# First transfers of a decoder layer: four of one k-tile and six of two, two of them issued by ScalarE, with joint splits and a 128-column warm-up source

## What is computed

```
h = einsum('bsd,de->bse', x, w_in)                 # x: 256 x 2048, w_in: 2048 x IN_WIDTH
q, k, v, z_attn, u_pool, z_pool, g_pre = split(h)
y_attn = mixed_dilated_attention(q, k, v) * silu(z_attn)
y_pool = causal_pool_mixer(u_pool) * silu(z_pool)
merged = sigmoid(..) * (y_attn @ w_proj_attn) + sigmoid(..) * (y_pool @ w_proj_pool)
out    = layer_norm(alpha * x + merged @ w_out)
```

## Time and profile before

| | |
|---|---|
| median of 3 runs | 939.66 us (939.53 to 940.01) |
| profiled execution | 939.67 us |
| span, first to last instruction | 937.9 us |
| TensorE busy | 930.7 us, 99% of the span |
| VectorE, ScalarE busy | 603.6 us, 399.6 us |
| mean granted TensorE clock | 0.999 |
| DMA | 180.77 MB, mean 193 GB/s |

### The profile page before, as it was taken

How to read it: one execution, slowest core, us unless ns; L and a number is a source line. 1 busy time by engine, 2 the same in 40 slices (tenths; PEclk the granted TensorE clock), 3 DMA queues, 4 the chain that set the end, 5 groups by cost and what they waited for, 6 DMA issues and landing times.

```text
span 937.9 us, 12269 instructions
## 1 busy us (share of the span) xinstructions
PE 930.7 (99%) x4838; PEld 796.9 (85%) x4838; DVE 603.6 (64%) x910; ACT 399.6 (43%) x533; POOL 0.2 (0%) x4
## 2 busy tenths in 40 slices
PE   9999999999999999999999999999999999999997
PEld 7888888888888888888888888888888888888887
DVE  6767657666777567557666768555555555556866
ACT  6444444444444344345344444444334433434340
POOL 0000000000000000000000000000000000000000
PEclk9999999999999999999999999999999999999999
DMA  9744544544545544544545546765565555557432
GB/s 375 265 158 176 207 180 150 207 162 170 204 156 181 183 174 164 202 180 155 203 160 194 185 175 244 256 227 193 180 210 195 202 179 186 203 209 257 179 135 90
DMA packets 26855, 180.77 MB, mean 193 GB/s; under 512 B 3247, under 2 KB 3503, under 8 KB 6191
## 3 DMA queue, kind: packets, MB, share of 16 engines
q1 hardware_dynamic: 25776, 173.71, 51.4%
q10 hardware_dynamic: 1028, 6.33, 1.8%
HBM read 177.93 MB, written 2.10 MB: 192 GB/s over the span
## 4 chain that ended last, share of the span: by engine, by line
PE 98%; DVE 1%; DMA 0%; ACT 0%; DVEq 0%; issue 0%
PE proj_ps L424 27%; PE proj_ps L430 14%; PE attn_ps L416 7%; PE attn_ps L417 7%; PE attn_ps L418 7%; PE value_ps L418 5%; PE value_ps L417 5%; PE value_ps L416 5%; PE proj_ps L417 3%; PE proj_ps L418 3%; PE proj_ps L416 3%; PE mixed_ps L418 3%; PE mixed_ps L417 3%; PE mixed_ps L416 3%; PE mixed_ps L553 1%; PE proj_ps L467 1%
## 5 line engine op out<-in xcount | busy, mean ns | idle before, releaser
L899 DVE TENSOR_TENSOR w_lo<-w_raw,w_hi 128x1024 fp32r<-128x1024 f32 x314 | 369.1, 1219 | 118.4 <-ACT w_hi L724 118.4
L724 ACT ACTIVATE w_hi<-w_raw 128x1024 fp32r<-128x1024 f32 x314 | 314.0, 1053 | 209.3 <-PE mixed_ps L418 76.3
L424 PE MATMUL proj_ps<-xt,w_hi 128*128 128x512 f32 x1088 | 378.9, 393 | 0.0
L430 PE MATMUL proj_ps<-xt,w_lo 128*128 128x256 f32 x1088 | 302.1, 280 | 0.0
L424 PEld LDWEIGHTS proj_ps<-xt,w_hi 128*128 128x128 f32 x1088 | 202.6, 187 | 44.1
L430 PEld LDWEIGHTS proj_ps<-xt,w_lo 128*128 128x128 f32 x1088 | 205.6, 189 | 1.4
L739 ACT ACTIVATE corr<-proj_ps 128x256 f32<-128x256 f32 x70 | 27.0, 385 | 205.8 <-PE proj_ps L430 203.0
L913 DVE TENSOR_TENSOR qk_f<-proj_ps,corr 128x256 f32<-128x256 f32 x46 | 19.5, 424 | 73.1 <-ACT corr L739 73.1
L418 PE MATMUL value_ps<-w_hi,xt 128*128 128x512 f32 x160 | 62.3, 390 | 0.0
L417 PE MATMUL value_ps<-w_lo,xt 128*128 128x512 f32 x160 | 62.3, 389 | 0.0
L416 PE MATMUL value_ps<-w_hi,xt 128*128 128x512 f32 x160 | 62.2, 389 | 0.0
(11 more groups left out here) (196 smaller groups left out, 1179.1 us busy)
## 6 DMA issues: line engine op xcount, KB each, us to landing
w_raw<-in_weights SPq DMA_DIRECT2D x158, 1024.0 KB, 4.8
first_raw<-in_first SPq DMA_DIRECT2D x8, 640.0 KB, 7.8
res<-in_x_rows ACTq DMA_DIRECT2D x1, 2048.0 KB
bias_rows<-in_gate_bias ACTq DMA_DIRECT2D x4, 512.0 KB, 4.7
out_rows<-res SPq DMA_DIRECT2D x8, 256.0 KB, 2.1
gamma<-in_gamma_row ACTq DMA_DIRECT2D x1, 1024.0 KB
beta<-in_beta_row ACTq DMA_DIRECT2D x1, 1024.0 KB
mask<-in_mask SPq DMA_DIRECT2D x1, 512.0 KB, 17.7
```

Source lines behind the costliest of these rows:

```text
L424: mm(bank, w_hi[:, slot, k * P:(k + 1) * P], tile.rearrange("p a s -> p (a s)"), start=first, stop=False)
L430: done = mm(bank[:, SEQ:2 * SEQ], w_lo[:, slot, k * P:(k + 1) * P], tile[:, 0, :], start=False, stop=last)
L724: activation(w_hi[:, slot, cols], w_raw[:, slot, cols], ACT.Copy).then_inc(hi_split, 1)
L899: tt(w_lo[:, slot, cols], w_raw[:, slot, cols], w_hi[:, slot, cols].bitcast(F32), ALU.subtract).then_inc(lo_split, 1)
```

## The change

The first transfers are cut into ten pieces: four of one k-tile (320 KB, rows of 2560 bytes) and six of two as before. Pieces 2 and 4 are issued by ScalarE, after it has waited for `zeros`, and run one activation on one column of it; the other eight are issued by SP in their order. ScalarE and VectorE split every piece jointly: one instruction for x and one of all three chunks for w. TensorE does, for the pieces of one k-tile, the w_hi matmuls of all three chunks and then their w_lo matmuls; for the pieces of two, w_hi and w_lo chunk by chunk as before, the last two pieces again chunk after chunk. The warm-up is 7 matmuls in place of 8, and each reads the same 128 columns of `zeros` four times, so that VectorE clears 128 columns and not 512.

```diff
--- before.py
+++ after.py
@@ -52,13 +52,14 @@
 RING = 3
 AHEAD = 2
 
-WARM_UP = 8
+WARM_UP = 7
 KEEP_UP = 10
 
-PIECES = tuple((k, k + 2) for k in range(0, KT, 2))
+SINGLES = 4
+BY_SCALAR = (2, 4)
+PIECES = tuple((k, k + 1) for k in range(SINGLES)) + tuple((k, k + 2) for k in range(SINGLES, KT, 2))
 ABREAST = RING
-SIDE_BY_SIDE = 6
-BY_CHUNK = 3
+SIDE_BY_SIDE = len(PIECES) - 2
 APART = (ABREAST - 1, ABREAST)
 PIECE_COLS = SEQ + ABREAST * P
 
@@ -349,28 +350,17 @@
             return piece_raw(q)[:, (upto - before) * SEQ:(upto - before) * PIECE_COLS].rearrange(
                 "p (n c) -> p n c", n=ABREAST)
 
-        def parts_of(q):
-
-            return [slice(n, n + 1) for n in range(ABREAST)] if q < BY_CHUNK else [slice(0, ABREAST)]
-
-        def x_parts_of(q):
-
-            before, upto = PIECES[q]
-            return [slice(k, k + 1) for k in range(before, upto)] if q == 0 else [slice(before, upto)]
-
-        def x_parts_done(k):
-            q = k // (PIECES[0][1] - PIECES[0][0])
-            return k + 1 if q == 0 else PIECES[0][1] + q
-
-        def parts_done(n, q):
-            return q * ABREAST + n + 1 if q < BY_CHUNK else BY_CHUNK * (ABREAST - 1) + q + 1
-
         def apart(j):
             return attn_ps[:, (j - APART[0]) * 512:(j - APART[0] + 1) * 512]
 
         def landed(eng, n, j, i, per):
 
             eng.wait_ge(raw_landed[(n + j) % RING], 16 * ((n + j) // RING) + i * (16 * per // RING))
+
+
+        def load_piece(eng, q):
+            lies = slice(P * PIECES[q][0] * PIECE_COLS, P * PIECES[q][1] * PIECE_COLS)
+            eng.dma_start(piece_raw(q), first_d[lies].rearrange("(p c) -> p c", p=P)).then_inc(piece_landed[q], 16)
 
 
         @block.sync
@@ -378,9 +368,9 @@
             def load(slot, chunk):
                 sp.dma_start(w_raw[:, slot, :], stream_d[chunk, :, :]).then_inc(raw_landed[slot], 16)
 
-            for q, (before, upto) in enumerate(PIECES):
-                lies = slice(P * before * PIECE_COLS, P * upto * PIECE_COLS)
-                sp.dma_start(piece_raw(q), first_d[lies].rearrange("(p c) -> p c", p=P)).then_inc(piece_landed[q], 16)
+            for q in range(len(PIECES)):
+                if q not in BY_SCALAR:
+                    load_piece(sp, q)
             for slot in range(RING):
                 load(slot, RING + slot)
             for dst, src in ((mask[:, :, :], mask_d), (ident[:, :], ident_d), (coef[:, :], coef_d),
@@ -461,13 +451,17 @@
             def first_part(n, q):
 
                 bank, ks = first_bank(n), range(*PIECES[q])
-                pe.wait_ge(piece_hi_done, parts_done(n, q))
+                pe.wait_ge(piece_hi_done, q + 1)
+                pe.wait_ge(x_lo_done, q + 1)
                 for k in ks:
-                    pe.wait_ge(x_lo_done, x_parts_done(k))
                     mm(bank, w_hi[:, n, k * P:(k + 1) * P], xt[:, k, :, :].rearrange("p a s -> p (a s)"),
                        start=(k == 0), stop=False)
-                pe.wait_ge(piece_lo_done, parts_done(n, q))
-                for k in ks:
+
+            def first_lo_part(n, q):
+
+                bank = first_bank(n)
+                pe.wait_ge(piece_lo_done, q + 1)
+                for k in range(*PIECES[q]):
                     done = mm(bank[:, SEQ:2 * SEQ], w_lo[:, n, k * P:(k + 1) * P], xt[:, k, 0, :],
                               start=False, stop=(k == KT - 1))
                 return done
@@ -475,11 +469,19 @@
             def first_chunks():
 
                 for q in range(SIDE_BY_SIDE):
-                    for n in range(ABREAST):
-                        first_part(n, q)
+                    if q < SINGLES:
+                        for n in range(ABREAST):
+                            first_part(n, q)
+                        for n in range(ABREAST):
+                            first_lo_part(n, q)
+                    else:
+                        for n in range(ABREAST):
+                            first_part(n, q)
+                            first_lo_part(n, q)
                 for n in range(ABREAST):
                     for q in range(SIDE_BY_SIDE, len(PIECES)):
-                        done = first_part(n, q)
+                        first_part(n, q)
+                        done = first_lo_part(n, q)
                     done.then_inc(chunk_done, 1)
 
             def scores(i):
@@ -559,7 +561,8 @@
 
             pe.wait_ge(zeros_ready, 1)
             for _ in range(WARM_UP):
-                mm(mixed_ps[:, :], zeros[:, 0:P], zeros[:, :], start=True, stop=True)
+                mm(mixed_ps[:, :].rearrange("p (a c) -> p a c", c=P), zeros[:, 0:P],
+                   zeros[:, 0:P].unsqueeze(1).broadcast_to([P, 512 // P, P]), start=True, stop=True)
             pe.sem_inc(chunk_done, FROM)
             def pool_map():
 
@@ -740,13 +743,14 @@
 
                 act.wait_ge(proj_free, FROM + banked(n, 0))
 
+            act.wait_ge(zeros_ready, 1)
+            activation(rstd[:, 4:5], zeros[:, 0:1].bitcast(F32), ACT.Copy)
+            for q in BY_SCALAR:
+                load_piece(act, q)
             for q, (before, upto) in enumerate(PIECES):
                 act.wait_ge(piece_landed[q], 16)
-                for k in x_parts_of(q):
-                    activation(xt[:, k, 0, :], piece_x(q)[:, k.start - before:k.stop - before, :],
-                               ACT.Copy).then_inc(x_hi_done, 1)
-                for n in parts_of(q):
-                    activation(w_hi[:, n, piece_cols(q)], piece_w(q)[:, n, :], ACT.Copy).then_inc(piece_hi_done, 1)
+                activation(xt[:, before:upto, 0, :], piece_x(q), ACT.Copy).then_inc(x_hi_done, 1)
+                activation(w_hi[:, :, piece_cols(q)], piece_w(q), ACT.Copy).then_inc(piece_hi_done, 1)
             act.sem_inc(hi_split, 2 * ABREAST)
 
             def exp_probs(i):
@@ -915,16 +919,14 @@
             def freed(n, j, i):
                 dve.wait_ge(proj_free, FROM + banked(n, j) + 1)
 
-            nc.vector.memset(zeros[:, :].bitcast(F32), 0.0).then_inc(zeros_ready, 1)
+            nc.vector.memset(zeros[:, 0:P].bitcast(F32), 0.0).then_inc(zeros_ready, 1)
             for q, (before, upto) in enumerate(PIECES):
-                for k in x_parts_of(q):
-                    dve.wait_ge(x_hi_done, x_parts_done(k.stop - 1))
-                    tt(xt[:, k, 1, :], piece_x(q)[:, k.start - before:k.stop - before, :],
-                       xt[:, k, 0, :].bitcast(F32), ALU.subtract).then_inc(x_lo_done, 1)
-                for n in parts_of(q):
-                    dve.wait_ge(piece_hi_done, parts_done(n.stop - 1, q))
-                    tt(w_lo[:, n, piece_cols(q)], piece_w(q)[:, n, :],
-                       w_hi[:, n, piece_cols(q)].bitcast(F32), ALU.subtract).then_inc(piece_lo_done, 1)
+                dve.wait_ge(x_hi_done, q + 1)
+                tt(xt[:, before:upto, 1, :], piece_x(q), xt[:, before:upto, 0, :].bitcast(F32),
+                   ALU.subtract).then_inc(x_lo_done, 1)
+                dve.wait_ge(piece_hi_done, q + 1)
+                tt(w_lo[:, :, piece_cols(q)], piece_w(q), w_hi[:, :, piece_cols(q)].bitcast(F32),
+                   ALU.subtract).then_inc(piece_lo_done, 1)
             dve.sem_inc(lo_split, 2 * ABREAST)
             for pad in (u_pad, pool_a, pool_b):
                 chain.add(nc.vector.memset(pad[:, 0:PAD], 0.0))
```

## The result

The changed kernel takes 941.85 us in the median of 9 runs (941.27 to 944.40), the kernel before 939.60 in 9 (939.49 to 940.01): 2.25 us more, a ratio of 1.0025 (95% interval 1.0015 to 1.0036). The slowest execution of before is 1.26 us faster than the fastest of the change, so the slowdown is real, where +0.4 us was forecast; 941.85 lies above the forecast's upper end of 941.0. The profiled execution took 941.39 us, 1.72 more than before's.

What follows compares the result with a forecast made beforehand. TensorE's progress through the first pieces was taken to bound the kernel. Piece 4 landing at 8.6 plus 4.05 gave 12.65 to 12.7 against 12.27, so 939.7 + 0.4 = 940.1 us, range 939.3 to 941.0.

Steps and rivals of the forecast that it cites:

- The bound: TensorE never idles from its first real matmul to 900 us, so delay in the first pieces moves the end equally.
- The start: First real matmul on TensorE at 5.0 us instead of 5.84, 0.8 us earlier, as the halved first piece lands at 4.1.
- L4 + 4.05: Time when TensorE is done with pieces 0 to 4: 4.05 us after piece 4 lands, against 12.27 before.
- L4: Landing time of piece 4, two k-tiles, the piece that decides; forecast 8.6 us, changing the total by L4 - 8.2 us.
- in perfect order, 8.1: Piece 4's landing if pieces arrive in order: 8.02 us plus 0 to 0.2 for smaller rows; a gain of 0.1 us.
- the meeting of the two queues: SP's and ScalarE's queues alternate packet by packet, so part of piece 5 overtakes piece 4, which lands at 8.6 us.
- the 2.5 of 8 rows assumed: Share of piece 5 taken to overtake piece 4: 2.5/8 of 1.58 us, added to 8.1.
- Order of issue: Rival, 0.12: DMA serves by issue time, piece 5 ahead of piece 4; landing 9.7 us, total 941.2, or 11.3 and 942.8.
- Warm-up at no cost: The shortened warm-up ends at 4.66 us instead of 5.40 and costs nothing while the real work is not ready.
- hides any clock trouble: TensorE's waits at piece 4 let it be late by up to 0.33 + 0.54 us before that costs anything.
- The 0.04 for slower: Chance given to a measurable slowdown of the whole kernel, beside 0.02 for faster and 0.94 for same.

Runs made afterwards that it cites:

- after_warm8: The changed kernel with 8 warm-up matmuls instead of 7: +1.93 us against the kernel before.
- sp_all: The changed kernel with all ten pieces issued by SP, none by ScalarE: +1.18 us against the kernel before.
- sp_paced: sp_all, with SP issuing a piece only when the piece four before it has landed, first weight chunks likewise: +0.22 us against the kernel before.
- odd_even: The kernel before with each of its first two pieces issued as two 320 KB transfers, even and odd partitions, rows of 5120 bytes: +0.79 us.
- small_rows: The kernel before with each of its first two pieces as one 640 KB transfer of 256 rows of 2560 bytes: +0.03 us.
- before_scalar: The kernel before, own 640 KB pieces and splits, with pieces 2 and 4 issued by ScalarE: +1.46 us.
- late_stream: sp_all, with SP waiting for piece 6 to land before issuing the first weight chunks and constants: +1.25 us against the kernel before.
- two_sp: Against the changed kernel: two one-k-tile pieces, then seven of two, all from SP, first two pairs split chunkwise, 8 warm-up matmuls: +1.31 us against the kernel before.
- halves: The kernel before with each of its first two pieces issued as two 320 KB transfers, lower and upper 64 partitions, rows of 5120 bytes: +3.00 us.

## Why the prediction was wrong

*The bound* was right: what TensorE gets through in the first pieces sets the end. Piece 5's first matmul moved by 1.77, 3.02 and 1.35 us in three profiles (the change, after_warm8, sp_all), the executions by 1.72, 2.97 and 1.23. sp_paced and odd_even ended 0.6 us earlier than that, by a stretch from 294 us on that the change does not touch.

*The start.* Forecast 5.0, measured 4.92; warm-up end 4.66 forecast, 4.78 measured.

*L4 + 4.05* held: 9.87 + 4.05 = 13.92 against 14.04.

*L4, the landing of piece 4, is the step that failed*: forecast 8.6, measured 9.87. These 1.3 us are the whole error of the profiled execution, 941.39 against 940.1. Both terms of L4 were too small.

The first is "in perfect order, 8.1". It took the stretch's 419 GB/s for transfers of half the size, with 0 to 0.2 us for the smaller rows. The rows cost nothing (small_rows), but with transfers of 320 KB single DMA engines fall behind, and in the kernels that issue everything from SP the rate falls too: 9.48 in sp_all, 1.4 us above the term. In the changed kernel late engines and supply make some 0.9 us by the landing events. The trace of before had no transfer of that size under load, so the bound from above should have been wide, and was not.

The second is the meeting of the two queues, forecast to add 0.5 us. In the changed kernel it made some 0.9 us by the landing events: as if more than half of piece 5 had gone ahead of piece 4 (0.9 of 1.58 us), not the 2.5 of 8 rows assumed. Taking it away won less, 0.4 us in the profiles, because sp_all lost more supply instead; between the medians it won 1.1. The mechanism, sharing packet by packet, is the one that was seen (before_scalar, 88 packets against 83), and it costs 1.5 us there without small transfers. ScalarE's issues went out at 1.41 and 1.83, while its table load ran, and not at 2.15 and 2.6 behind it.

*Order of issue*, the slower rival, named 9.7 for L4 and 941.2 us and came nearest in numbers, but not by its mechanism: piece 5 did not go ahead of piece 4, they moved together.

*Warm-up at no cost, "hides any clock trouble"* held for the change's profile, whose first k-tiles did run at the slow level (1.19 us for two matmuls at 4.92) while TensorE had to wait later anyway. Alone, the same edit costs 1.5 us in the median, which the prediction did not see.

*The range* left out what decides: it bounded the order of the pieces but not how late single engines are. The 0.04 for slower should have been several times that.

What stays open is why smaller transfers let single engines fall behind. Rows and the loads behind are ruled out, and SP issues a piece each 0.5 us, faster than one of 320 KB moves (0.79). The size of a transfer is not told apart from the number under way at once: fewer under way helps but does not cure. Open, too, is why the rate fell with all pieces from SP and hardly with two queues; that is one execution of each.

## What to carry to other kernels

Cutting the first transfer gives an early start, but where the next transfers are already at full rate, the end is set by when the whole of the first few is there, and smaller transfers made exactly that later. Don't count on a second issuing engine for speed, and keep pieces that are needed in order in one queue. When a transfer is late, look at the bytes moved by then as well: here they were nearly as many as before, and belonged to the wrong pieces. Don't add up what two causes cost alone; taking one away let the other grow. Repeat a kernel often enough to see whether its times fall in groups: an idle TensorE between a warm-up and the work may cost nothing in one execution and 2 us in the next.

## What was not expected of the hardware

- From SP alone, transfers of 320 KB moved at 270 (sp_all) and 324 GB/s (odd_even; 262 in late_stream, 366 in two_sp) in a stretch where those of 640 KB moved at 397 to 411, with rows of 2560 or 5120 bytes alike. The changed kernel, with two pieces from ScalarE, moved 389 there. The landing events of the 16 engines spread over 1.7 to 2.7 us at the worst piece instead of 0.8 (the change, sp_all, late_stream, two_sp).
- Two transfers of 64 neighbouring partitions each ran at 227 GB/s, two of every second partition at 324 (4.0 to 6.5 us).
- The granted-clock column reads 1.00 in the first microseconds though the matmuls' starts, 0.43 us apart, show the 1.2 GHz level. Later falls it does show: in halves TensorE idled 1.89 us before its real work, and the windows 7.2 to 8.2 and 8.3 to 11.2 have the clock in the third column from the right:

```profile
7.20:8.20 1.00, 0.98 (x5) 0.83 (x6) 1.00 (x4) 0.58 (x2) 0.00 (x0) 1.00 0.90 200
8.30:11.20 2.90, 2.39 (x9) 1.82 (x7) 0.93 (x3) 1.54 (x5) 0.00 (x0) 0.50 0.97 374
```

- DMA issues of ScalarE ran beside its own table load (0.74 to 2.02):

```profile
1.41 0.86 ACTq L363 DMA_DIRECT2D first_raw<-in_first  x2
```
